# Four weight units of each later expert pair loaded as transfers of 112, 8 and 8 partitions instead of one of 128

## The chip, the cores and the metric

The kernel runs on one core of one Trainium2 chip. The metric is the device time of one execution in microseconds (us), lower being better. The kernel before has a median of 1338.05 us over three runs (1337.34 to 1338.09).

## What is computed

Two layers on a sequence of 256 tokens with 1024 features, all in float32. The first layer is a gated linear recurrence followed by a dense SwiGLU of inner width 3584. The second is a forgetting attention followed by a mixture of eight SwiGLU experts, of which each token uses two. The change touches only that last part:

```python
def moe_swiglu(h, router, w_gate, w_up, w_down):
    logits = (t @ router).astype(jnp.float32)
    top_v, top_i = lax.top_k(logits, TOP_K)             # TOP_K = 2 of N_EXPERTS = 8
    w = jax.nn.softmax(top_v, axis=-1)
    combine = jnp.sum(jax.nn.one_hot(top_i, N_EXPERTS) * w[..., None], axis=1)
    for e in range(N_EXPERTS):
        out = out + combine[:, e:e + 1] * swiglu(t, w_gate[e], w_up[e], w_down[e])
```

Each expert has a gate and an up matrix of 1024 x 3584 and a down matrix of 3584 x 1024, 14 MiB each, so the eight experts are 336 MiB of weights, each read once.

## The kernel before

The front of the kernel (the recurrence, the dense part and the attention) streams its weights in 1 MiB units through six places called `raw` and takes up to about 500 us. The experts come after it. Their tokens are gathered by routing into groups of 32 slots: a "large" expert of a pair has three groups, a "small" one two. Experts are worked in pairs, four pairs for this input: an opening pair, a second one, one in a loop and a last one, each described by an object `Group`.

An expert's weights are read in units of 128 rows by 3584 floats (14,336 bytes in each of 128 partitions, 1.75 MiB). There are eight units for the gate matrix ("G"), eight for up ("U") and eight for down ("D"; `PARTS` is 8). Within the list of a pair (`UNITS`, 48 entries, built by `pair_units`) the kinds alternate, with the down units of the pair's small expert postponed into the next pair. After the last pair a list of eight down units remains (`LAST_UNITS`).

The units go through a ring of eight places (`RING`, `PERMANENT`; three more are used in the opening). The order is strict. SyncE runs `pair_loads`: for each unit it waits until TensorE has finished with the place (`used` against `group.free(i)`), then `load` issues one DMA of the whole unit. That DMA adds 16 to the semaphore `arrived` of its place when it has landed. SyncE does nothing else in this part until the output. TensorE takes the units in the same order: `summed` for a gate or up unit, `lowered` for a down unit. Each starts with a wait on `arrived` of its place against `group.landed(i)`, then issues the unit's matmuls and adds one to `used` at the end of the last one. For each group of slots a gate or up unit is multiplied in four strips of 512 + 384 columns; a down unit is multiplied in pieces of 256 columns. ScalarE and VectorE apply the activation and the routing weights between the stages. The program is written out by hand in this order; no planner places anything.

The wait that the transfer ends, in `summed` and `lowered` alike (lines 1251 and 1267), and the issue itself (line 420):

```python
pe.wait_ge(arrived[group.slot(i)], group.landed(i))
...
sp.dma_start(dst, src).then_inc(arrived[group.slot(i)], 16)
```

Of the kernel before, what the change touches and what calls it, by code (L numbers as in the profile page):

```python
# [22 lines left out]
P = 128  # L23
# [68 lines left out]
def at(count, per, i):  # L92

    return count if i is None else i * per + count
# [7 lines left out]
def pair_units(opening):  # L102

    def sums(kind, job):
        return [(kind, job, n) for n in range(KT)]
    early, late = (range(EARLY), range(EARLY, PARTS))
    return (sums("G", LARGE) + ([] if opening else downs(EARLIER, early)) + sums("U", LARGE)
            + ([] if opening else downs(EARLIER, late)) + sums("G", SMALL) + downs(LARGE, early)
            + sums("U", SMALL) + downs(LARGE, range(EARLY, PARTS)))


OPENING_UNITS, UNITS = pair_units(True), pair_units(False)
LAST_UNITS = downs(EARLIER, range(PARTS))
PAIR_UNITS = len(UNITS)
assert PAIR_UNITS % RING == 0 and len(OPENED) == RING + 3


class Group:


# [20 lines left out]
    def slot(self, i):  # L141
        n = self.later(i)
        return OPENED[n] if n < 0 else PERMANENT[n % RING]

    def landed(self, i):
        n = self.later(i)
        return 16 if n < 0 else at(16 * (n // RING + 2), 16 * PAIR_UNITS // RING, self.i)
# [21 lines left out]
def hybrid_trunk(nc, x, norm_mix, norm_ffn, lru_w_in, lru_conv_w, lru_conv_b, lru_w_a, lru_b_a, lru_w_x, lru_b_x,  # L169
                 lru_log_lambda, lru_w_out, fox_w_in, fox_b_f, fox_q_gain, fox_k_gain, fox_w_out, ffn_w_gate,  # L170
                 ffn_w_up, ffn_w_down, moe_router, moe_w_gate, moe_w_up, moe_w_down, out):
    with ExitStack() as ctx:
        def sem(name):
            return ctx.enter_context(nc.semaphore(name))
# [124 lines left out]
        def strip(c):  # L299
            return slice(c * SLOTS, (c + 1) * SLOTS)  # L300
# [47 lines left out]
            sem(s) for s in ("m_act", "m_aT", "m_acc", "m_S", "m_Sw", "m_col", "m_tab", "m_fin"))  # L348
        arrived = [sem(f"arrived{i}") for i in range(len(OPENED))]
        out_done, sumsq_v, par_in2, ff_T = sem("out_done"), sem("sumsq_v"), sem("par_in2"), sem("ff_T")  # L350
        h_f_done, xn_act = sem("h_f_done"), sem("xn_act")


# [42 lines left out]
        @block.sync  # L396
        def _(sp):
            for t in range(TT):
                sp.dma_start(X[:, t], x[0, t * P:(t + 1) * P, :]).then_inc(x_in, 16)
            for load in par_loads[4:]:  # L400
                sp.dma_start(*load).then_inc(par_in2, 16)
            for n, (w, rows, col) in enumerate(front_units()):
                if n == RR:
                    sp.wait_ge(used, 1)
                elif n > RR:
                    sp.wait_ge(lo_done, max(m for m in range(n) if DENSE[m] == DENSE[n]))
                sp.dma_start(raw[:, DENSE[n]].rearrange("p (k n) -> p k n", k=UK), unit_of(w, rows, col)
                             ).then_inc(landed[DENSE[n]], 16)
                if n == 4:
                    sp.dma_start(wax[:, 0], lru_w_a[0].rearrange("h i j -> i h j")).then_inc(wax_in, 16)  # L410
                    sp.dma_start(wax[:, 1], lru_w_x[0].rearrange("h i j -> i h j")).then_inc(wax_in, 16)

            def load(group, i, expert):
                kind, job, n = group.table[i]
                dst = places[group.slot(i)]
                if kind == "D":
                    src = expert_w[2][expert].rearrange("o (p r) n -> p (o r n)", r=ROWS)[:, n * PLACE:(n + 1) * PLACE]
                else:
                    src = expert_w["GU".index(kind)][expert, n * P:(n + 1) * P, :].rearrange("o p n -> p (o n)")
                sp.dma_start(dst, src).then_inc(arrived[group.slot(i)], 16)  # L420

            def pair_loads(group):
                experts = {LARGE: slice(FIRST, FIRST + 1)} if group is OPENING else {}
                for i, (kind, job, n) in enumerate(group.table):
                    if group is OPENING and i < len(OPENED):
                        continue
                    if job not in experts:
                        if group is OPENING:
                            sp.wait_ge(listed, 1)
                        col = group.col(-1) + 1 if job == EARLIER else group.col() + job  # L430
                        experts[job] = bass.ds(sp.value_load(ids[0:1, bass.ds(col, 1)], min_val=0, max_val=E - 1), 1)
                    sp.wait_ge(used, group.free(i))
                    load(group, i, experts[job])

            def dense_done(*places):
                for place in places:
                    n = last_dense(place)
                    if place < RR:
                        sp.wait_ge(lo_done, n)
                    else:  # L440
                        sp.wait_ge(used, n + 1)

            def open_unit(i):
                load(OPENING, i, slice(FIRST, FIRST + 1))

            dense_done(2, 3, 4, 5)
            open_unit(0)
            open_unit(1)
            sp.wait_ge(scored, 8)
            open_unit(2)  # L450
            dense_done(0, 1, 2)
            open_unit(3)
            sp.wait_ge(o_T, 4)
            open_unit(4)
            dense_done(11, 12)
            open_unit(5)
            dense_done(6, 7)
            open_unit(6)
            dense_done(7, 8, 9)
            open_unit(7)  # L460
            dense_done(9, 10, 11)
            open_unit(8)
            sp.wait_ge(routed, 1)
            open_unit(9)
            sp.wait_ge(hn_hi_done, 2)
            sp.wait_ge(hn_lo_done, 2)
            open_unit(10)
            pair_loads(OPENING)
            pair_loads(SECOND)
            sp.wait_ge(counted, 1)  # L470
            loops = sp.value_load(nblk_i[0:1, 0:1], min_val=LOOPS, max_val=LOOPS_MAX)
            with sp.Fori(0, loops) as n:
                pair_loads(Group(n, 2))
            pair_loads(Group(loops, 2))
            pair_loads(Group(loops, 3, LAST_UNITS))
            for n in range(4):
                j, t = n // 2, n % 2
                sp.wait_ge(m_fin, n + 1)
                sp.dma_start(out[0, t * P:(t + 1) * P, j * CW:(j + 1) * CW], X[:, t, j * CW:(j + 1) * CW]
                             ).then_inc(out_done, 16)  # L480
            sp.wait_ge(out_done, 64)
# [348 lines left out]
        def _(pe):  # L830
# [416 lines left out]
            def summed(group, kind, job, n):  # L1247

                i = group.place[kind, job, n]
                w = places[group.slot(i)]  # L1250
                pe.wait_ge(arrived[group.slot(i)], group.landed(i))
                for a in range(GROUPS[job]):
                    if n == 0:
                        acc_free(group, kind, job, a)
                    x = xg[:, n, FIRST_SLOT[job] + a * SLOTS:FIRST_SLOT[job] + (a + 1) * SLOTS]
                    for b, first, width in PIECES:
                        for c in range(STRIPS):
                            ins = mm(ps[strip(c), 2 * a + b, 0:width], x, w[:, c * STRIP + first:c * STRIP + first + width],  # L1258
                                     start=n == 0, stop=n == KT - 1, skip_group_check=True)
                    if n == KT - 1 and a < GROUPS[job] - 1:  # L1260
                        ins.then_inc(m_part, 1)
                ins.then_inc(used, 1)

            def lowered(group, job, n):

                i, small = group.place["D", job, n], min(job, SMALL)
                pe.wait_ge(arrived[group.slot(i)], group.landed(i))
                at_place = n * PLACE
                for r in range(at_place // D, (at_place + PLACE) // D):
                    for a in range(GROUPS[small]):  # L1270
                        for c in range(STRIPS):
                            at_row = r * D + c * QUARTER
                            held_in = i if at_row >= at_place else i - 1
                            first = at_row - at_place + (i - held_in) * PLACE
                            ins = mm(ps[strip(c), 6 + a // 2, quarter(a % 2)], aTs[small][:, r, held(a)],  # L1275
                                     places[group.slot(held_in)][:, first:first + QUARTER],
                                     start=r == 0 and a % 2 == 0, stop=r == ROWS - 1, skip_group_check=True)
                    if r * D < at_place:
                        ins.then_inc(used, 1)
                if (at_place + PLACE) % D == 0:  # L1280
                    ins.then_inc(used, 1)
# [684 lines left out]
```

## Time and profile before

| | before |
|---|---|
| median of three runs | 1338.05 us |
| profiled execution, device time | 1338.2 us |
| its span, first to last instruction | 1336.4 us |
| granted TensorE clock, mean | 0.998 |
| PE busy | 1271.3 us (95%) |
| LDWEIGHTS busy | 766.0 us (57%) |
| DVE, ACT, POOL busy | 363.3, 284.5, 30.9 us |
| DMA | 435.53 MB, mean 326 GB/s |
| HBM read, written | 432.69 MB, 1.05 MB |
| chain that ended last | PE 73%, DMA 23%, ACT 2%, DVE 1% |

The device time holds the span and about 2 us around it. Busy shares are of the span. The rates of the DMA row are those of all 16 DMA engines together; "share of 16 engines" is the time that packets took, over 16 times the stretch, and it can come out slightly over 100% as packets overlap at their ends.

### The profile page before, as it was taken

The numbers are of one execution on the slowest core, as the hardware profiler recorded it, in microseconds if no ns is written. First come the engines' busy times: TensorE is split into PE (matmuls) and PEld (weight loads), VectorE is DVE, ScalarE is ACT, GpSimd is POOL, SyncE is SP. The second block draws the span as 40 slices with busy tenths as digits, with TensorE's granted clock in tenths as the row PEclk, the third lists the DMA queues.
The fourth block names the chain that finished last, engine by engine and source line by source line (L and its number), as shares of the span: only waits on it lengthen the run. The fifth ranks groups of instructions, "written<-read, shape, count | busy, mean of one in ns | idle before, by whom it ended". The sixth has DMA issues, their size and how long they took to land.

```text
span 1336.4 us, 27795 instructions
## 1 busy us (share of the span) xinstructions
PE 1271.3 (95%) x12897; PEld 766.0 (57%) x12897; DVE 363.3 (27%) x470; ACT 284.5 (21%) x357; POOL 30.9 (2%) x34
## 2 busy tenths in 40 slices
PE   7999999999999999999999999899998799989897
PEld 7978888888888884335534434344344254344344
DVE  6976444445654363020100200100110100020010
ACT  5855444443545530000000000000000000000000
POOL 2000000000230000000000000000000000000000
PEclk9999999999999999999999999999999999999999
DMA  9556555554441298899999999999999999999994
GB/s 338 171 167 227 185 184 184 188 188 157 157 127 64 87 424 339 319 401 425 426 425 425 425 425 425 427 424 426 426 424 426 426 425 426 425 425 425 425 425 198
DMA packets 70323, 435.53 MB, mean 326 GB/s; under 512 B 4656, under 2 KB 6816, under 8 KB 45632
## 3 DMA queue, kind: packets, MB, share of 16 engines
q1 hardware_dynamic: 69744, 433.10, 81.0%
q8 instruction: 101, 1.65, 0.5%
q0 software_dynamic: 368, 0.63, 0.2%
q14 instruction: 14, 0.11, 0.0%
q10 hardware_dynamic: 96, 0.03, 0.0%
HBM read 432.69 MB, written 1.05 MB: 325 GB/s over the span
## 4 chain that ended last, share of the span: by engine, by line
PE 73%; DMA 23%; ACT 2%; DVE 1%; issue 1%; SPq 0%; POOL 0%; DVEq 0%; ACTq 0%
PE ps L1258 25%; DMA ring<-in_moe_w_down_dram 16%; PE ps L1275 13%; PE ps L839 9%; PE ps L841 9%; PE ps L840 9%; DMA ring<-in_moe_w_gate_dram 6%; PE ps L1229 1%; PE ps L1069 1%; PE ps L1096 1%; PE ps L855 1%; PE ps L881 1%; PE ps L871 1%; PE ps L868 1%; PE ps L870 1%
## 5 line engine op out<-in xcount | busy, mean ns | idle before, releaser
L1258 PE MATMUL ps<-ring,xg 128*32 128x512 f32 (+1 forms) x4384 | 423.1, 540 | 26.6 <-DMA ring<-in_moe_w_up_dram 16.1
L1258 PEld LDWEIGHTS ps<-ring,xg 128*32 128x32 f32 x4384 | 140.1, 110 | 299.6 <-issue 251.3
L1423 DVE TENSOR_TENSOR wlo<-raw,whi 128x2048 fp32r<-128x2048 f32 x73 | 166.5, 2287 | 74.2 <-PE ps L841 72.2
L541 ACT ACTIVATE whi<-raw 128x2048 fp32r<-128x2048 f32 x73 | 139.3, 1916 | 85.3 <-PE ps L841 83.8
L839 PE MATMUL ps<-whi,hT_hi 128*128 128x512 f32 x384 | 153.4, 399 | 2.4 <-DVE wlo L1423 1.4
L841 PE MATMUL ps<-whi,hT_lo 128*128 128x512 f32 x384 | 149.9, 390 | 0.0
L840 PE MATMUL ps<-wlo,hT_hi 128*128 128x512 f32 x384 | 149.7, 390 | 0.0
L1275 PE MATMUL ps<-ring,aTL 128*32 128x256 f32 x2352 | 133.9, 380 | 7.3 <-DMA ring<-in_moe_w_down_dram 7.1
L1903 DVE TENSOR_TENSOR gtL<-gtL,ps 128x896 f32<-128x896 f32 x12 | 13.1, 1089 | 368.3 <-PE ps L1258 368.3
L1275 PEld LDWEIGHTS ps<-ring,aTL 128*32 128x32 f32 x2352 | 77.6, 110 | 59.8 <-DMA ring<-in_moe_w_down_dram 7.8
L1275 PE MATMUL ps<-ring,aTS 128*32 128x256 f32 x1568 | 90.2, 380 | 10.7 <-DMA ring<-in_moe_w_down_dram 9.7
L839 PEld LDWEIGHTS ps<-whi,hT_hi 128*128 128x128 f32 x384 | 72.2, 188 | 18.3 <-issue 3.1
L841 PEld LDWEIGHTS ps<-whi,hT_lo 128*128 128x128 f32 x384 | 72.1, 188 | 15.3
L840 PEld LDWEIGHTS ps<-wlo,hT_hi 128*128 128x128 f32 x384 | 72.3, 188 | 13.7
L1275 PEld LDWEIGHTS ps<-ring,aTS 128*32 128x32 f32 x1568 | 51.9, 110 | 46.9 <-DMA ring<-in_moe_w_down_dram 14.1
L1258 PE MATMUL ps<-ring_last,xg 128*32 128x512 f32 (+1 forms) x592 | 58.5, 540 | 3.2 <-DMA ring_last<-in_moe_w_up_dram 3.2
L1903 DVE TENSOR_TENSOR gtS<-gtS,ps 128x896 f32<-128x896 f32 x8 | 8.7, 1087 | 176.3 <-PE ps L1258 176.3
L795 ACT ACTIVATE yS<-ps 128x512 f32<-128x512 f32 x4 | 2.4, 597 | 217.1 <-PE ps L1275 217.1
L839 PE MATMUL ps<-whi,fT_hi 128*128 128x512 f32 x112 | 44.9, 401 | 0.0
L840 PE MATMUL ps<-wlo,fT_hi 128*128 128x512 f32 x112 | 44.3, 395 | 0.0
L841 PE MATMUL ps<-whi,fT_lo 128*128 128x512 f32 x112 | 44.3, 395 | 0.0
L1258 PEld LDWEIGHTS ps<-ring_last,xg 128*32 128x32 f32 x592 | 18.8, 110 | 40.2 <-issue 34.9
(292 smaller groups left out, 1016.9 us busy)
## 6 DMA issues: line engine op xcount, KB each, us to landing
ring<-in_moe_w_down_dram SPq DMA_DIRECT2D x56, 1792.0 KB, 29.1
ring<-in_moe_w_gate_dram SPq DMA_DIRECT2D x55, 1792.0 KB, 27.5
ring<-in_moe_w_up_dram SPq DMA_DIRECT2D x55, 1792.0 KB, 24.8
raw<-in_fox_w_in_dram SPq DMA_DIRECT2D x16, 1024.0 KB, 5.4
raw<-in_ffn_w_gate_dram SPq DMA_DIRECT2D x14, 1024.0 KB, 5.1
raw<-in_ffn_w_up_dram SPq DMA_DIRECT2D x14, 1024.0 KB, 5.1
raw<-in_ffn_w_down_dram SPq DMA_DIRECT2D x14, 1024.0 KB, 5.1
ring_last<-in_moe_w_up_dram SPq DMA_DIRECT2D x8, 1792.0 KB, 27.3
```

The costliest lines, as they stand in the source:

```text
L541: nc.scalar.activation(whi[:, m % HR], raw[:, DENSE[m]], ACT.Copy).then_inc(hi_done, 1)
L839: mm(dst(t), hi, whi[:, m % HR, k * CW:(k + 1) * CW], start=first and k == 0, stop=False)
L840: mm(dst(t), hi, wlo[:, m % LR, k * CW:(k + 1) * CW], start=False, stop=False)
L841: ins = mm(dst(t), lo, whi[:, m % HR, k * CW:(k + 1) * CW], start=False, stop=last and k == UK - 1)
L855: ins = mm(dst, raw[:, 0, k * CW + c * P:k * CW + (c + 1) * P], h_f[:, k], start=k == 0 and c % 2 == 0, stop=False, skip_group_check=True)
L868: mm(dst, wh, hT_hi[:, kk], start=half == 0 and k == 0 and c % 2 == 0, stop=False, skip_group_check=True)
L870: mm(dst, wh, hT_lo[:, kk], start=False, stop=False, skip_group_check=True)
L871: ins = mm(dst, wl, hT_hi[:, kk], start=False, stop=half == 1 and k == UK - 1, skip_group_check=True)
L1258: ins = mm(ps[strip(c), 2 * a + b, 0:width], x, w[:, c * STRIP + first:c * STRIP + first + width], start=n == 0, stop=n == KT - 1, skip_gr ...
L1275: ins = mm(ps[strip(c), 6 + a // 2, quarter(a % 2)], aTs[small][:, r, held(a)], places[group.slot(held_in)][:, first:first + QUARTER], sta ...
L1423: nc.vector.tensor_tensor(wlo[:, m % LR], raw[:, DENSE[m]], whi[:, m % HR].bitcast(F32), ALU.subtract).then_inc(lo_done, 1)
L1903: nc.vector.tensor_tensor(gts[job][:, a], gts[job][:, a], of_group(a), ALU.mult).then_inc(m_act, 1)
```

## The change

Within the lists of the second, the looped and the last pair, the units at places 0, 12, 24 and 36 are loaded by three DMAs. The first carries partitions 0 to 111 and adds to `arrived` as before. The other two carry partitions 112 to 119 and 120 to 127 and add 16 each to one new semaphore, `rest_in`. TensorE waits for both semaphores before such a unit. All other units, those of the opening pair and the eight after the last pair are loaded as before. The bytes and their places in memory are the same.

```diff
+UNEVEN = range(0, PAIR_UNITS, 12)
+TOP, STEP = 112, 8
...
+    def uneven(self, i):
+        return self.table is UNITS and i in UNEVEN
+
+    def rest(self, i):
+
+        per = 16 * (P - TOP) // STEP
+        return at(per * (len(UNEVEN) * (self.ahead - 1) + UNEVEN.index(i) + 1), per * len(UNEVEN), self.i)
...
+        rest_in = sem("rest_in")
...
-                sp.dma_start(dst, src).then_inc(arrived[group.slot(i)], 16)
+                if not group.uneven(i):
+                    sp.dma_start(dst, src).then_inc(arrived[group.slot(i)], 16)
+                    return
+                sp.dma_start(dst[0:TOP], src[0:TOP]).then_inc(arrived[group.slot(i)], 16)
+                for p in range(TOP, P, STEP):
+                    sp.dma_start(dst[p:p + STEP], src[p:p + STEP]).then_inc(rest_in, 16)
...
                 pe.wait_ge(arrived[group.slot(i)], group.landed(i))
+                if group.uneven(i):
+                    pe.wait_ge(rest_in, group.rest(i))
```

The last two lines stand in `summed` and in `lowered`.

## Rows read from the trace of the kernel before

**Rows 1.** the page's 40 slices of 33.4 us; digits are tenths busy

```profile
PE   7999999999999999999999999899998799989897
...
PEclk9999999999999999999999999999999999999999
DMA  9556555554441298899999999999999999999994
GB/s 338 171 167 227 185 184 184 188 188 157 157 127 64 87 424 339 319 401 425 426 425 425 425 425 425 427 424 426 426 424 426 426 425 426 425 425 425 425 425 198
```

**Rows 2.** the page's DMA queues: packets, MB, share of 16 engines' time

```profile
q1 hardware_dynamic: 69744, 433.10, 81.0%
q8 instruction: 101, 1.65, 0.5%
```

**Rows 3.** transfers, 600 to 1300 us: packets by size, then the queues

```profile
DMA packets 23343, 297.66 MB, mean 425 GB/s; under 512 B 2588, under 2 KB 2588, under 8 KB 2588
...
q1 hardware_dynamic: 23269, 296.49, 100.1%
q8 instruction: 69, 1.13, 0.7%
```

**Rows 4.** TensorE's waits, 600 to 1300 us: total us, times, longest us

```profile
PE ps L1258 <- DMA ring<-in_moe_w_up_dram: 16.1, 14, 1.4
PE ps L1275 <- DMA ring<-in_moe_w_down_dram: 12.5, 14, 1.5
PE ps L1258 <- DMA ring<-in_moe_w_gate_dram: 10.5, 12, 1.4
PE ps L1258 <- DMA ring_last<-in_moe_w_up_dram: 3.2, 3, 1.1
```

**Rows 5.** chain of waits, 500 to 1336 us: start us, us, what

```profile
777.96 30.98 DMA ring<-in_moe_w_down_dram
...
987.14 32.24 DMA ring<-in_moe_w_down_dram
...
1197.50 31.06 DMA ring<-in_moe_w_down_dram
```

**Rows 6.** end of the chain, 1170 to 1336 us, same columns

```profile
1296.10 29.33 DMA ring<-in_moe_w_down_dram
...
1325.47 3.71 PE ps L1275 x64
...
1333.22 0.66 DVE X L1937 x2
```

**Rows 7.** stretches of 2 us at the end; last columns DMA share, GB/s

```profile
1306.00:1308.00 2.00, 2.00 (x40) 1.19 (x40) 0.00 (x0) 0.00 (x0) 0.00 (x0) 1.00 1.01 430
1308.00:1310.00 2.00, 2.00 (x45) 1.18 (x37) 0.00 (x0) 0.00 (x0) 0.00 (x0) 1.00 0.67 287
1310.00:1312.00 2.00, 2.00 (x44) 1.23 (x40) 0.00 (x0) 0.00 (x0) 0.00 (x0) 1.00 0.54 223
...
1320.00:1322.00 2.00, 1.38 (x29) 0.60 (x24) 0.00 (x0) 0.00 (x0) 0.00 (x0) 1.00 0.54 216
1322.00:1324.00 2.00, 1.85 (x36) 0.85 (x28) 0.00 (x0) 0.00 (x0) 0.00 (x0) 1.00 0.27 115
1324.00:1326.00 2.00, 0.53 (x12) 0.35 (x16) 0.00 (x0) 0.00 (x0) 0.00 (x0) 1.00 0.03 14
```

**Rows 8.** the tile ring: one issue's ns min/median/max, and us to landing

```profile
L420 SPq DMA_DIRECT2D ring<-in_moe_w_down_dram x56: 328/333/339, 583.8 to 1296.1; - x56
...
DMA to landing us min/median/max: 7.1/27.9/32.5
```

**Rows 9.** SyncE's waits, 600 to 1300 us: total us, times, longest us

```profile
SPq L420 <- PE ps L1258: 387.0, 107, 7.2
SPq L420 <- PE ps L1275: 222.2, 56, 8.1
```

**Rows 10.** a transfer of 8 partitions at the start, in the whole span's issues

```profile
par_rows<-in_lru_conv_b_dram ACTq DMA_DIRECT2D x1, 4.0 KB
```

More of the change, by code:

```diff
@@ L1267, in lowered @@
                 pe.wait_ge(arrived[group.slot(i)], group.landed(i))
+                if group.uneven(i):
+                    pe.wait_ge(rest_in, group.rest(i))
                 at_place = n * PLACE
```

## The prediction

> **What bounds the kernel now.** I read the page's slices first. From slice 18 on (about 600 us) the DMA row is 9 in every slice and the rate stands at 424 to 427 GB/s up to the last slice, while PE swings between 8 and 9 [rows 1]. The clock row is 9 throughout, so the clock plays no part. The queues come second: one queue (q1, the SyncE issues) carries 433.10 MB of the whole span's traffic, and beside it stands a small instruction queue, q8, with 101 packets and 1.65 MB [rows 2]. In 600 to 1300 us, q1 fills 100.1% of the time of the 16 DMA engines [rows 3]. Nothing is left there to be better overlapped: more bytes per us can't be had on average.
>
> TensorE is close behind. In the same 700 us it waits for weight landings only 16.1 + 12.5 + 10.5 + 3.2 = 42.3 us, in 43 short waits of at most 1.5 us [rows 4], so each pair of experts ends with the weight stream and TensorE has about 12 us to spare in each. The chain of waits then goes in a loop: TensorE frees a place, SyncE issues, and the transfer lands 31 to 32 us later; at 128 rows over 16 engines (4.34 us, worked out below) that is seven units deep in the queue. The same point of the pair recurs in it at 777.96, 987.14 and 1197.50 us, every 209.2 and 210.4 us [rows 5]. The last of it is a transfer of the down weights that lands at 1325.43 us, and TensorE starts at once (1325.47); behind it comes a fixed tail of 1336.4 - 1325.4 = 11.0 us [rows 6].
>
> The row that matters for this change comes last. If all 16 engines were in step, the DMA share would fall from 1 to 0 within a few us at the end of the stream. It does not: it is 1.01 in 1306 to 1308, falls to 0.67 and then stands at 0.54 to 0.49 down to 1322, with 0.27 and 0.03 after that [rows 7]. So half of the engines, eight, run out of work at about 1309.5, and the other eight go on until 1322 to 1325. The gap is about 1322 - 1309.5 = 12.5 us. Yet every transfer gives each engine the same bytes: 128 rows, one packet each (23343 - 2588 packets for 297.66 MB, 14.34 KB each, is a weight row of 3584 floats) [rows 3]. The likely load on only eight of them is the instruction queue: 69 packets in 700 us at 0.7% of 16 engines' time [rows 3], 78 us in all, or 1.14 us each. On eight engines that is 9.8 us each in 700 us, which is about the gap that has built up. It is a reading, since no row says on which engine a packet ran. A unit is usable only when its slowest engine has landed, so the kernel pays the slow eight's time.
>
> **The change part by part.** The price of one row on one engine: 16 x 700 x 1.001 us over 296.49 MB / 14336 B = 20,682 rows is 0.542 us [rows 3], so a unit takes 8 x 0.542 = 4.34 us.
>
> *Rows moved between engines.* A 128-row transfer gives each engine 8 rows. 112 rows over 16 engines give 7. A transfer of 8 rows can occupy at most eight engines, with one row each. If the two short ones both take the same eight (call them the short-transfer eight), those carry 9 rows of such a unit and the others 7. Places 0, 12, 24 and 36 of the 48 units of a pair are cut so, in the three pairs after the opening one: 12 units. So the one eight gains 12 x 0.542 = 6.5 us of work and the other loses 6.5 us.
> By a rule of the Trainium skill (DMA: Bandwidth & Descriptors, "Why a DMA increments its semaphore by 16 and not by 1") a transfer runs on the largest number of engines up to 16 that divides its outermost dimension, and takes the lowest-numbered ones, which would be 16 for 112 rows and the same first eight for both short transfers. No run here shows it yet.
> If the eight that lose rows are the slow eight, their end goes from 1325.4 to 1318.9, and the others' from 1309.5 to 1312.5 (with a spread of 3 us like that of the slow eight) up to 1316 to 1319. The two meet, and the last landing comes earlier by half the gap, 12.5 / 2 = 6.2 us: 1319.2. If they are the fast eight, the end goes 6.5 us later. For what comes in between I take -6.2 and keep both signs.
>
> *Does the gain reach the end?* TensorE has 42.3 us of waits to give in 600 to 1300 [rows 4], seven times the gain, and the last wait before the tail is one for a landing [rows 6]. All the time from the first cut unit to the last lies in the full stretch [rows 1]. The gain grows by about 2.1 us per pair, so every landing wait shrinks evenly. What is late next is the other eight: their lead is used up almost exactly, and one more cut unit would bring nothing.
>
> *Two more issues per cut unit.* An issue on SyncE takes 0.333 us [rows 8]: 24 more are 8.0 us, beside 387.0 + 222.2 us in which SyncE waits for TensorE in the 700 us [rows 9]. The short transfers are issued 0.33 and 0.67 us after the long one, and the median transfer lands 27.9 us after its issue [rows 8], behind six others, so the queue hides it. Cost 0; with the cover gone it would be 12 x 0.67 = 8.0 us.
>
> *More semaphore packets and one more wait.* Each transfer ends in a small packet on each of its engines (2588 under 512 B in 700 us [rows 3], 16 per 128-row unit). A cut unit adds 16 on the short-transfer eight. The 0.542 us per row above already holds one such packet for eight rows, so were all of the difference between a row's share and its bytes theirs, it would stay far under a row: 24 of them on each engine of that eight cost between 0 and, at an eighth of a row (0.07 us), 1.6 us. I take 0, since they fall on engines with a lead. The added TensorE wait is satisfied with or before the unit's own landing, as the short rows are queued right behind the long part; 12 waits of 0.04 us, the chain's usual "issue" step, would be 0.5 us, and less than nothing can't come of it. I take 0.
>
> *The row's own price.* All rows above come from transfers of 128 partitions, where 16 engines reach all of them at full rate. The only few-partition transfers of the trace are the parameter loads at the start, 4 KB for 8 partitions, with no landing time of its own [rows 10]. So the cost of an 8-row transfer of 112 KB is bounded from below by 0.542 us (each row on its own engine at full rate) and from above by eight rows one after the other, 4.3 us. The long part is bounded by 7 x 0.542 = 3.8 us and by twice that, should pairs of engines meet on the same partitions. I take the lower ends, being the only durations that the trace has, and keep the upper for a rival.
>
> **Sum.** Against the profiled execution (1338.2 us, span 1336.4): -6.2 + 0 + 0 + 0, so 1332.0, and against the median of 1338.05, 1331.9 us.
>
> **The rivals.**
> (A) Short transfers share their way into memory; slower. Eight rows that go to neighbouring partitions may have to take turns, four engines at a time. Then each of the two short transfers holds its eight engines 4 x 0.542 = 2.2 us in place of 0.54, 3.25 us more per cut unit, 39 us over 12. The point from which it decides: the short-transfer eight have about 6.2 us each to give, 0.5 us per cut unit; one row time more per unit and the gain is gone. In full it gives -6.2 + 39 = +33, 1371 us; with engines that are out of step by 1 to 3 us (the last landings spread over 1322 to 1325 [rows 7]) about half, +13, 1351 us. If the long part meets conflicts too, up to 45 us more. For it: nothing in the rows excludes it. Against it: in the full stretch the rate doesn't dip though engines drift apart by up to 12 us [rows 1, 7], but there each engine has rows of its own, so that says little.
> A page of the Trainium skill speaks for it (SBUF — State Buffer, "Door 1: The DMA port swizzle"): partitions are reached through 16 ports in groups of four, and a transfer gets no more rate than its ports, about 27 GB/s each, so that 8 neighbouring partitions have two ports. Its figure would make a short transfer 8 x 14336 B / 54 GB/s = 2.1 us by estimate.
> (B) The wrong eight; slower. If the instruction packets ride on the short-transfer eight, the slow end grows by 12 x 0.542: 1344.6 us. The rows can't tell; the size of the shift, which is just half the gap, suits the right side but proves nothing.
> (C) No difference. The short transfers are spread over all engines, or half of (A) eats the gain: 1337 to 1339. For it: the trace shows no transfer that leaves engines out.
>
> **How the numbers follow.** The forecast, right eight and full-rate rows: 0.46, at 1331.9, itself between 1330 and 1335. (A) 0.30, most of it at 1342 to 1370. (B) 0.11. (C) 0.13. About 0.2% (2.7 us) is what a measurement can tell here, so faster than 1335.4 is 0.47, slower than 1340.7 0.40, between 0.13. The range of 1330 to 1362 holds the forecast, (C), (B) and the milder two thirds of (A).
>
> **What would show it.** After the change: in the end stretches the DMA share stays near 1 until about 1316 and then falls to 0 within 3 us, with no plateau at 0.5; the last landing is near 1319; the pair period is near 207 to 208 us; TensorE's waits shrink by about 6 us. A plateau of some 25 us would be (B). Under (A) q1's rate in 600 to 1300 falls below 420 GB/s while its share stays at 100%, and waits appear at the cut units, of 2 us and more. I am wrong if the time is above 1335.4.

## The result and the profile after

The changed kernel took 1490.97 us (median of four runs, 1484.72 to 1501.9) against 1337.69 us (1336.94 to 1338.09) for the kernel before on the same chip: ratio 1.1155, with an interval of 1.1087 to 1.1224. It is 153 us slower, or 12.8 us for each of the twelve cut units. The profiled execution took 1493.51 us, its span 1491.8 us.

The page after, in the parts that answer to [rows 1, 2]:

```profile
PE 1316.5 (88%) x12897; PEld 777.9 (52%) x12897; DVE 362.7 (24%) x470; ACT 284.7 (19%) x357; POOL 30.9 (2%) x34
...
PEclk9999999999999999999898999989899899989999
DMA  9465565644316989999999999999999999999992
GB/s 341 143 201 194 184 198 183 196 147 153 100 53 277 403 309 363 425 347 425 331 380 356 310 410 285 388 313 331 370 300 384 277 374 289 348 340 338 373 418 119
...
q1 hardware_dynamic: 69936, 433.10, 82.4%
q8 instruction: 101, 1.65, 0.5%
...
PE 53%; DMA 42%; DVE 2%; ACT 2%; issue 1%; SPq 0%; POOL 0%; DVEq 0%; ACTq 0%
```

Bytes and instruction fetches are as before. The DMA row is still 9 everywhere, yet the rate, a flat 425 GB/s before, falls to between 277 and 388 in most slices. DMA's part of the chain has gone from 23% to 42%. The queues in 600 to 1450 us, against [rows 3]:

```profile
DMA packets 23662, 299.25 MB, mean 352 GB/s; under 512 B 2796, under 2 KB 2796, under 8 KB 2796
...
q1 hardware_dynamic: 23588, 298.09, 100.0%
q8 instruction: 68, 1.11, 0.6%
```

Busy for 100.0% of the time at 352 GB/s instead of 425: engines never lack work, their packets take longer. That is worth 850 x (1 - 352/425) = 146 us of the 155 by which the profiled execution is longer (1493.5 against 1338.2 us). TensorE's waits in 600 to 1490 us, which answer to [rows 4] (L1278 is the old L1258, L1297 the old L1275):

```profile
PE ps L1297 <- DMA ring<-in_moe_w_down_dram: 70.2, 32, 6.3
PE ps L1278 <- DMA ring<-in_moe_w_up_dram: 36.2, 18, 5.6
PE ps L1278 <- DMA ring<-in_moe_w_gate_dram: 26.6, 10, 5.9
```

Single waits are up to 6.3 us long, against 1.5 us before. Short stretches of the changed kernel show where the rate is lost (columns as in [rows 7]; the last three are granted clock, DMA share and GB/s). The first cut unit is issued at 640.21 us, the second at 694.80, the fifth at 882.53, the ninth at 1153.19, the twelfth at 1354.36:

```profile
640.00:656.00 16.00, 16.00 (x204) 7.85 (x200) 5.77 (x4) 0.70 (x1) 0.00 (x0) 1.00 1.01 425
...
660.00:664.00 4.00, 4.00 (x56) 3.01 (x52) 0.00 (x0) 0.70 (x1) 0.00 (x0) 1.00 0.93 201
664.00:668.00 4.00, 4.00 (x80) 2.37 (x76) 0.00 (x0) 0.00 (x0) 0.00 (x0) 1.00 1.02 204
...
656.00:672.00 16.00, 15.65 (x268) 9.71 (x259) 0.00 (x0) 1.00 (x2) 0.00 (x0) 1.00 1.01 243
672.00:712.00 40.00, 40.00 (x460) 17.98 (x464) 0.00 (x0) 3.27 (x4) 0.00 (x0) 1.00 1.00 424
712.00:732.00 20.00, 10.94 (x156) 5.48 (x148) 0.00 (x0) 0.00 (x0) 0.00 (x0) 0.83 1.01 253
...
896.00:928.00 32.00, 24.86 (x368) 15.16 (x368) 3.96 (x3) 2.22 (x3) 0.00 (x0) 0.95 1.00 261
...
1156.00:1200.00 44.00, 34.36 (x444) 17.60 (x436) 5.64 (x4) 1.58 (x3) 0.00 (x0) 0.88 1.01 278
...
1360.00:1376.00 16.00, 7.05 (x68) 2.11 (x64) 0.00 (x0) 1.83 (x2) 0.00 (x0) 0.89 1.00 236
1376.00:1384.00 8.00, 7.59 (x144) 4.69 (x139) 0.00 (x0) 0.00 (x0) 0.00 (x0) 1.00 1.00 389
1384.00:1396.00 12.00, 11.05 (x224) 6.72 (x212) 0.00 (x0) 0.60 (x1) 0.00 (x0) 1.00 1.01 287
```

Every cut unit leaves a dip. The first two begin 16 and some 20 us after the issue, when the unit's turn in the queue comes; the twelfth begins only some 6 us after it and ends some 42 us after it. So by then some engines reach a unit soon after its issue, and others much later. At the floor of a dip the rate is some 200 GB/s, half of 425, with all 16 engines busy. After the first dip it is back at 424. The rate missing in a dip gives its cost: the first, 16 x (425 - 243)/425 = 6.9 us; the second, 20 x (425 - 253)/425 = 8.1; the fifth (896 to 928), 32 x (425 - 261)/425 = 12.3; the ninth (1156 to 1200), 44 x (425 - 278)/425 = 15.2; the twelfth, 7.1 + 0.7 + 3.9 = 11.7 from the last three rows. So later cuts cost about twice the first, and the twelfth dip has two humps, which begin 24 us apart.

The end, against [rows 6, 7]:

```profile
1454.00:1456.00 2.00, 1.56 (x31) 0.70 (x24) 0.00 (x0) 0.00 (x0) 0.00 (x0) 1.00 1.00 423
1458.00:1460.00 2.00, 2.00 (x40) 1.45 (x36) 0.00 (x0) 0.00 (x0) 0.00 (x0) 1.00 0.47 195
1462.00:1464.00 2.00, 2.00 (x44) 1.23 (x40) 0.00 (x0) 0.00 (x0) 0.00 (x0) 1.00 0.21 87
1470.00:1472.00 2.00, 0.74 (x16) 0.17 (x8) 0.00 (x0) 0.00 (x0) 0.00 (x0) 1.00 0.18 79
1478.00:1480.00 2.00, 1.29 (x24) 0.52 (x16) 0.00 (x0) 0.00 (x0) 0.00 (x0) 1.00 0.07 29
```

```profile
1451.11 29.60 DMA ring<-in_moe_w_down_dram
...
1480.75 3.70 PE ps L1297 x64
...
1488.49 0.66 DVE X L1959 x2
```

Most engines now run dry near 1458, but three of 16 (0.18 to 0.21) go on to the last landing at 1480.71: the gap is some 23 us, against 16 before (1309.5 to 1325.4). These 7 us and the 146 of the lower rate make 153 of the 155. The tail behind the last landing is the old 11 us.

### The profile page after: what moved, and what is told of

Read it like the earlier page. It is cut to its first block, busy times and chain, and to the rows that moved or that the text cites. A ratio compares the mean times of both kernels' runs of the same rounds, so it can differ in the third digit from the quotient of the medians.

```text
span 1491.8 us, 27864 instructions
## 1 busy us (share of the span) xinstructions
PE 1316.5 (88%) x12897; PEld 777.9 (52%) x12897; DVE 362.7 (24%) x470; ACT 284.7 (19%) x357; POOL 30.9 (2%) x34
## 4 chain that ended last, share of the span: by engine, by line
PE 53%; DMA 42%; DVE 2%; ACT 2%; issue 1%; SPq 0%; POOL 0%; DVEq 0%; ACTq 0%
PE ps L1278 20%; DMA ring<-in_moe_w_up_dram 17%; DMA ring<-in_moe_w_gate_dram 16%; DMA ring<-in_moe_w_down_dram 9%; PE ps L857 8%; PE ps L859 8%; PE ps L858 8%; PE ps L1297 3%; PE ps L1087 1%; DVE wlo L1445 1%; PE ps L1114 1%; PE ps L899 0%; PE ps L1210 0%; PE ps L1318 0%; PE ps L976 0%
## 5 line engine op out<-in xcount | busy, mean ns | idle before, releaser
L1278 PE MATMUL ps<-ring,xg 128*32 128x512 f32 (+1 forms) x4384 | 444.9, 563 | 74.7 <-DMA ring<-in_moe_w_up_dram 36.2
L1278 PEld LDWEIGHTS ps<-ring,xg 128*32 128x32 f32 x4384 | 147.4, 114 | 363.4 <-issue 305.2
L1297 PE MATMUL ps<-ring,aTL 128*32 128x256 f32 x2352 | 139.5, 391 | 21.6 <-DMA ring<-in_moe_w_down_dram 21.5
L1297 PE MATMUL ps<-ring,aTS 128*32 128x256 f32 x1568 | 103.0, 414 | 36.2 <-DMA ring<-in_moe_w_down_dram 35.2
L1297 PEld LDWEIGHTS ps<-ring,aTL 128*32 128x32 f32 x2352 | 79.2, 113 | 78.5 <-DMA ring<-in_moe_w_down_dram 17.5
L1297 PEld LDWEIGHTS ps<-ring,aTS 128*32 128x32 f32 x1568 | 54.9, 119 | 82.0 <-DMA ring<-in_moe_w_down_dram 39.5
L1278 PE MATMUL ps<-ring_last,xg 128*32 128x512 f32 (+1 forms) x592 | 58.5, 540 | 4.0 <-DMA ring_last<-in_moe_w_up_dram 4.0
L818 ACT ACTIVATE ST<-ps 128x768 f32<-128x768 f32 (+1 forms) x8 | 5.6, 704 | 185.6 <-PE ps L1338 185.6
## 6 DMA issues: line engine op xcount, KB each, us to landing
ring<-in_moe_w_gate_dram SPq DMA_DIRECT2D x49, 1792.0 KB, 33.4
```

Of the source, the lines that this page charges most:

```text
L818: nc.scalar.activation(ST[:, first:first + n].rearrange("p a t -> p (a t)"), flat(4, n * T), ACT.Copy).then_inc(m_ST, 1)
```

## The experiments

Each edit is against the changed kernel. Runs whose names begin with e are the kernel with another form of loading; m1 and m2 are programs that only load. The kernel before had medians of 1337.19, 1338.16 and 1337.75 us beside the three sets of runs, in which the experiments stand as e1 to e4; e5 to e7 and m1; e8, e10, e11 and m2.

**Two short transfers as one, and equal halves.**

```diff
-TOP, STEP = 112, 8
+TOP, STEP = 112, 16      # e1
+TOP, STEP = 64, 64       # e2
```

> The 12 cut units are loaded as 112 + 16 partitions, with no transfer of 8. If the long part is what costs (seven rows per engine no longer lie where eight did, so that engines meet on the same partitions' way into memory), most of the 153 us stays: 1430 to 1490 us, with dips of the DMA rate to 200-300 GB/s at every cut unit. If the two short transfers on eight engines cost (my rival A in its first form, 39 us), the dips go and the time is 1338 to 1350 us, since 112 + 16 gives every engine 8 rows again.

> The 12 cut units are loaded as two transfers of 64 partitions. Every engine still gets 8 rows and there is one more issue per unit. If what counts is only rows per engine and the number of transfers, nothing changes: 1336 to 1341 us. If engines share ways into memory, and 64 neighbouring partitions reach only half of the ways, each half runs at half rate: at least 4.3 us more per cut unit, 12 x 4.3 = 52 us, and more when the engines are out of step: 1390 to 1450 us.

e1 took 1473.06 us, +136; e2 took 1493.94 us, +157, above the 1450 that I gave as its upper end. Each is one run, but the differences are far above what a run varies. With one short transfer less, nearly all of the loss remains; with no short transfer at all, and eight rows on each engine, it is all there. So the eight-row transfers are not the main cost, nor is the uneven number of rows.

**The long part alone.** The two short transfers and their wait are taken out; 16 rows of each of the 12 units are not loaded.

> The change without the two short transfers: at the 12 places only partitions 0 to 111 are loaded, 16 rows of each are left out. It moves 12 x 0.54 = 6.5 us less per engine. If the long part alone makes the cost: 1450 to 1475 us, near the 1473 of 112 + 16 less a few us. If the short transfers hold up the rest by their 2.1 us rows (as they do alone): 1400 us or less.

1450.58 us, one run: +113 though 12 units are an eighth smaller, which is worth 12 x 0.542 = 6.5 us. The long part by itself makes about three quarters of the loss.

**Two transfers, cut in other directions.** e5 cuts by columns (all 128 partitions in each half), e8 takes every second partition (64 in each, as e2 has).

```diff
# e5
+sp.dma_start(dst[:, 0:WHOLE], src[:, 0:WHOLE]).then_inc(arrived[group.slot(i)], 16)
+sp.dma_start(dst[:, WHOLE:], src[:, WHOLE:]).then_inc(rest_in, 16)
# e8
+sp.dma_start(dst[0:P:2], src[0:P:2]).then_inc(arrived[group.slot(i)], 16)
+sp.dma_start(dst[1:P:2], src[1:P:2]).then_inc(rest_in, 16)
```

> At the 12 places the unit comes in two transfers of all 128 partitions and half of the columns each: as many transfers, issues and bytes per transfer as 64 + 64 partitions, and rows half as long. If cutting a unit in two costs by itself (issue, semaphore packets, shorter packets), a good part of the 157 us of 64 + 64 shows here. If only the partitions of a transfer count: 1337 to 1340 us, below 2 us more.

> At the 12 places the unit comes in two transfers of 64 partitions, the even ones and the odd ones, in place of 0-63 and 64-127 (1493.9 us). If a shape that runs at full rate alone (64 partitions two apart took 31.3 us for 14) costs nothing here either: 1337 to 1341 us. If each engine must write where it does in whole units, or it meets the others once they are out of step: 1345 to 1400 us.

e5: 1338.53 us, ratio 1.0003 (0.9993 to 1.0013). e8: 1338.09 us, ratio 1.0003 (0.9993 to 1.0013). The same 16 us, in which the first cut unit passes, in e2 and then in e8:

```profile
656.00:672.00 16.00, 14.80 (x252) 9.15 (x240) 0.00 (x0) 1.51 (x2) 0.00 (x0) 1.00 0.99 231
```

```profile
656.00:672.00 16.00, 16.00 (x272) 10.06 (x268) 0.00 (x0) 1.02 (x2) 0.00 (x0) 1.00 1.00 421
```

231 against 421 GB/s, with two transfers of 64 rows, one more issue and one more wait in both. Cutting in two costs nothing; which partitions stand together in a transfer decides. Each transfer reads from HBM the rows of the partitions that it writes, here and in all runs, so no run tells the writing side from the reading side. Against the reading side speaks only that whole down units, whose pieces lie 114,688 bytes apart in memory, stream at the same 425 GB/s as gate and up units, whose pieces lie side by side [rows 1].

**The shapes by themselves.** m1 only loads: thirteen phases of 14 units (the last of 7), each drained before the next, with nothing else on the chip's queues.

> Only loads, no computing: the program runs thirteen phases of loads of the expert weights (rows of 14,336 bytes) one after the other and copies x to the output; everything else is left out. Each phase issues 14 transfers of one shape to 14 places and waits for all. By rows per engine alone (0.542 us a row): 128 partitions 61 us, 112 53 us, 0-63 30 us, 0-95 46 us, 8 neighbours 7.6 us (112-119), 8 partitions four apart 7.6 us (0-28 and 64-92), 4 neighbours 7.6 us, 4 partitions four apart 7.6 us, 64 partitions two apart 30 us, 8 partitions sixteen apart 7.6 us; then seven cut units of 112 + 8 + 8, 30 to 34 us. If four neighbouring partitions (and those 32 further) share one way into memory at one engine's rate: 128 still 61 us and the partitions four apart still 7.6 us, but 0-63 61 us, 8 neighbours 30 us, 4 neighbours 30 us, 8 sixteen apart 15 us, and 112 between 61 and 107 us.

Its steady stretches (columns: POOL busy, clock, DMA share, GB/s), in order: partitions 0 to 127; 0 to 111; 0 to 63; 0 to 95; 112 to 119; then 0 to 28 by fours; 0 to 3; 0 to 126 by twos; seven cut units of 112 + 8 + 8.

```profile
10.00:60.00 50.00, 0.00 (x0) 1.00 1.01 429
75.00:145.00 70.00, 0.00 (x0) 1.00 1.01 275
160.00:210.00 50.00, 0.00 (x0) 1.00 1.01 208
225.00:290.00 65.00, 0.00 (x0) 1.00 1.01 248
300.00:325.00 25.00, 0.00 (x0) 1.00 0.47 50
328.00:338.00 10.00, 0.00 (x0) 1.00 0.41 138
...
355.00:380.00 25.00, 0.00 (x0) 1.00 0.24 25
...
462.00:490.00 28.00, 0.00 (x0) 1.00 0.95 405
...
510.00:572.00 62.00, 0.00 (x0) 1.00 0.90 200
```

With a share of 1.01, all 16 engines busy, 112 partitions get 275 GB/s, 96 get 248, the lower 64 get 208, and 64 taken by twos 405. Eight neighbours keep half of the engines busy (0.47) for 50 GB/s; eight partitions four apart, at much the same share, get 138, and there SyncE, with 0.7 us per issue, may set the pace. Four neighbours get 25 GB/s, so two groups of four get 50. Per unit, the 112 rows take 1.606 MB / 275 = 5.8 us, against 7 x 0.542 = 3.8. An eight-row transfer takes 0.115 MB / 50 = 2.3 us, against 0.542. A whole cut unit takes 1.835 MB / 200 = 9.2 us, against 4.3: +4.9. Alone, then, the two short transfers lose more (3.5 us) than the long one (2.0).

A page of the Trainium skill (SBUF — State Buffer, "Door 1: The DMA port swizzle") has partitions in groups of four on 16 ports of some 27 GB/s, with partitions 32 apart on the same port, so that 0 to 63 reach half of the ports and get at most about 218 GB/s. The 208, 50 and 25 GB/s above agree with it.

**Fewer cuts.** e7 cuts only the unit at place 0 of the three pairs (`UNEVEN = range(0, 12, 12)`).

> The change with only place 0 of each later pair cut (3 units instead of 12). If each cut unit costs the same, 153 / 4 = 38 us more: about 1376 us. If a cut costs more the further the engines have drifted apart, and the cuts themselves drive them apart, less than a quarter: 1350 to 1368 us.

1369.79 us, one run: +31.6, or 10.5 us per cut. Its three dips:

```profile
656.00:672.00 16.00, 15.04 (x256) 9.36 (x251) 0.00 (x0) 1.51 (x2) 0.00 (x0) 1.00 1.00 226
868.00:892.00 24.00, 18.45 (x293) 11.68 (x291) 0.00 (x0) 2.22 (x3) 0.00 (x0) 1.00 1.00 239
1084.00:1116.00 32.00, 24.61 (x368) 14.75 (x368) 4.11 (x3) 2.22 (x3) 0.00 (x0) 0.95 1.01 242
```

The rate missing is worth 7.5, 10.5 and 13.8 us, and their sum of 31.8 is the whole loss. The same three units cost 6.9, 12.3 and 15.2 us in the changed kernel, where three more cuts lie between each and the next. So a cut costs more the later it comes, and most of that growth is there without the cuts between. The kernel before has half of its engines 16 us ahead at the end; a lead that builds up through the stream would explain the growth, but only its end is seen.

**Engines out of step.** m2 only loads: phases of six whole units, X and five whole ones, with X whole, 112 + 8 + 8, 112 + 16, or by twos; each once in step and once after 16 rows that only eight of the engines carry.

> Only loads again; everything else is left out. Eight phases: 6 whole units, one unit loaded in some form, 5 whole units; the form is whole, 112 + 8 + 8, 112 + 16, or two transfers of every second partition; each once with all engines in step, and once after 16 rows that only eight engines carry (partitions four apart, 8.6 us), so that those start late. From the shapes alone: whole 12 x 4.4 = 53 us, 112 + 8 + 8 4.7 us more, 112 + 16 about 3.8 us more, every second partition 0 to 0.2 us more; started late, each 8.6 us longer. If a cut costs the same whatever the engines' lags, the started-late phases exceed the whole one (61.6 us) by the same 4.7, 3.8 and 0.2 us. If engines out of step meet on each other's partitions for as long as the lag lasts, they exceed it by more: 8 us and above for 112 + 8 + 8, and some us even for every second partition.

The first phase is issued from 0.73 us on. SyncE's first issues of the second to the fifth:

```profile
55.23 15.19 SPq L193 DMA_DIRECT2D place<-in_moe_w_gate_dram  x22
```

```profile
122.56 14.92 SPq L193 DMA_DIRECT2D place<-in_moe_w_gate_dram  x14
```

```profile
182.83 15.36 SPq L193 DMA_DIRECT2D place<-in_moe_w_gate_dram  x23
```

```profile
257.69 16.25 SPq L193 DMA_DIRECT2D place<-in_moe_w_gate_dram  x13
```

In step, the whole unit's phase lasts 54.5 us and the cut one's 182.83 - 122.56 = 60.3, +5.8. Out of step they last 67.3 and 74.9, +7.5. The same differences for 112 + 16 are +5.1 and +7.2, and by twos +0.1 and -1.4. The lead was to be 16 x 0.542 = 8.7 us. But SyncE issued the 16 short transfers 0.7 us apart, slower than a row's 0.542, so the eight engines nearly kept up: the held-back whole phase is 12.8 us longer than the other, and not 8.7. A lead of 8.7 us would show at its end as a plateau of 0.5 (columns as for m1):

```profile
119.00:120.00 1.00, 0.00 (x0) 1.00 0.61 258
120.00:121.00 1.00, 0.00 (x0) 1.00 0.14 57
121.00:122.00 1.00, 0.00 (x0) 1.00 0.10 43
```

So a lead of at most some 2 us was made. Even so a cut out of step costs some 2 us more, and one that lines up costs nothing more. The direction is the one that the kernel shows; a lead of 12 us and more was never given to a stream without TensorE.

**Which eight are late.** e3 replaces place 36 of three pairs by eight transfers of eight rows, four apart, within partitions 0 to 63; e10 by eight of six rows. The rest of those three units is left out.

```diff
+for n, b in enumerate((0, 1, 2, 3, 32, 33, 34, 35)):
+    rows = slice(b, b + 29, 4)        # e3;  b + 21 in e10
+    sp.dma_start(dst[rows], src[rows]).then_inc(rest_in if n else arrived[group.slot(i)], 16)
```

> Which eight engines lag? In one unit of each of the three later pairs (place 36) partitions 64 to 127 are not loaded at all, and partitions 0 to 63 come in eight transfers of 8 partitions, four apart (0, 4, ... 28 and so on). The short-transfer eight then carry 8 rows as before, the others none: 3 x 8 x 0.542 = 13 us less for those. If those others are the lagging eight (as my forecast had it), the end comes up to the lead of 12.5 us earlier: 1325 to 1328 us. If the short-transfer eight lag, nothing is won: 1337 to 1340 us. If 8-row transfers are slow even with partitions four apart, it is above 1345 us.

> As the run with the upper half left out (1336.2 us), but with transfers of 6 partitions four apart, 8 of them, so that only six engines carry 8 rows of the unit at place 36 and the other ten none (80 of its 128 rows are not loaded). In that earlier run the last two of 16 engines lagged as before, so two of the lagging engines must be among the short-transfer eight. If they are its last two, all lagging engines are relieved now by 3 x 8 rows = 13 us: 1325 to 1329 us. If they are among its first six, 1336 to 1338 us again.

e3: 1336.18 us, ratio 0.9991 (0.9981 to 1.0). e10: 1335.29 us, ratio 0.9981 (0.9972 to 0.9991). The end of e3, then of e10:

```profile
1308.00:1310.00 2.00, 2.00 (x44) 1.20 (x40) 0.00 (x0) 0.00 (x0) 0.00 (x0) 1.00 0.62 259
1310.00:1312.00 2.00, 2.00 (x44) 1.07 (x37) 0.00 (x0) 0.00 (x0) 0.00 (x0) 1.00 0.24 100
...
1320.00:1322.00 2.00, 2.00 (x44) 1.07 (x36) 0.00 (x0) 0.00 (x0) 0.00 (x0) 1.00 0.12 50
```

```profile
1310.00:1312.00 2.00, 2.00 (x41) 1.20 (x41) 0.00 (x0) 0.00 (x0) 0.00 (x0) 1.00 0.12 50
...
1320.00:1322.00 2.00, 1.37 (x28) 0.54 (x19) 0.00 (x0) 0.00 (x0) 0.00 (x0) 1.00 0.07 29
```

Half the load of three units, 24 rows or 13 us, is taken from the eight engines that these rows don't use (fourteen eight-row transfers in a row held a share of 0.47 in m1, so they keep to the same eight). Had all eight late engines been among them, the plateau of 0.54 in [rows 7] would be gone. It falls to 0.12, two of 16. So six of the late engines were relieved, and two carry the eight-row transfers. With six rows per transfer, a share of 0.07 is left at 1320, one of 16. If transfers of six rows run on six of the same eight engines, which no row shows, one late engine is among those six and the other is one of the remaining two. Little was won in time (1.0 and 2.5 us), since a unit is usable only when its last engine has landed.

**A balanced cut.** e4 loads columns 0 to 1791 of place 36 in one transfer, and the rest in 16 transfers of eight partitions four apart; e6 uses eight neighbours instead.

```diff
+sp.dma_start(dst[:, 0:WHOLE], src[:, 0:WHOLE]).then_inc(arrived[group.slot(i)], 16)
+for b in [h + b for h in (0, 32, 64, 96) for b in range(4)]:     # e6: for b in range(0, P, 8)
+    rows = slice(b, b + 29, 4)                                    # e6: slice(b, b + 8, 1)
+    sp.dma_start(dst[rows, WHOLE:], src[rows, WHOLE:]).then_inc(rest_in, 16)
```

> The same balance as my forecast wanted, without a transfer of 112: at place 36 of the three later pairs, columns 0 to 1791 of the unit come in one transfer of 128 partitions, and the other half of the columns in 16 transfers of 8 partitions, four apart. The short-transfer eight carry 12 rows' worth, the others 4; over three units 12 rows = 6.5 us are moved. If an engine's rows are its only cost, -6 us: 1331 to 1333 us. If each way into memory is already full with the rows of the engine that owns it, what the short-transfer eight write for the others slows those by as much as it relieves them: no gain, 1338 to 1350 us. 56 and more transfers of slow issue would show as idle DMA engines, not expected.

> As the run with the columns apart (1356 us), but each of the 16 short transfers takes 8 neighbouring partitions instead of 8 that lie four apart. Same bytes, same engines by number, same issues. By the engines alone: 1356 us again. If neighbours share a way into memory, each short transfer takes 4 rows' time instead of one, half a row each: 16 x 3 x 0.27 = 13 us more on eight engines per cut unit, 39 us over three: 1380 to 1400 us.

e4: 1356.29 us, ratio 1.0146 (1.0129 to 1.0163), so 6 us per such unit and above both of the ranges expected. e6: 1361.25 us in one run, 5 us more, between its two. In e4 the engines are never idle (share 1.01 from 600 to 1300 us) but get 418 and then 416 GB/s, which is worth 14 of the 19 us. My reading is that the short-transfer eight then write also to partitions that the other eight serve; it isn't separated from the rows of half the length. e6 costs far less than full turn-taking would; SyncE's 16 issues may set the pace there, which wasn't separated either.

## Why the prediction was wrong

The forecast was 1331.9 us, in a range of 1330 to 1362; measured was 1491. Rival (A) had the right kind of mechanism, transfers that don't reach their full rate, but laid it on the wrong part, and its price was off too.

- *What bounds the kernel.* Right: the stream of weights sets the time. TensorE's waits for landings went from 42 us (600 to 1300) to 133 us (600 to 1490) in the groups shown, and the end moved by what the stream lost.
- *The row's own price: the failed step.* "I take the lower ends, being the only durations that the trace has." The long part was taken at 7 x 0.542 = 3.8 us; alone it takes 5.8. A short transfer was taken at 0.542 us; alone it takes 2.3. The bounds written beside them, 7.6 and 4.3 us, hold both of these prices. The reason given for the lower ends was no reason: every row of the trace is a 128-partition transfer, so none is near to the new shapes. But the prices alone would have given only 1338 - 6 + 12 x 4.9 = 1391 us, and even both upper bounds, 11.3 us more per cut unit, stay under the 12.8 measured. The sum had no term for the whole units that share the stream with a cut one; that is the other 100 us.
- *Rival (A)* laid the cost on the short transfers (+39), with the long part as an afterthought of "up to 45". In the kernel it is the other way round: e11 has about 113 of the 153 us with the long part alone. And even the two together, 84 us, fall short of 153, since they count only the cut unit's own rows. The fifth dip passes 32 x 261 = 8.4 MB, four and a half units, below the full rate, so whole units next to a cut one are slowed as well: the first dip costs 6.9 us, later ones 8 to 15.
- *"With engines that are out of step ... about half".* Wrong in sign. I thought that a lead keeps rows from meeting. What the runs show is that whole units, halves by columns (e5) and every second partition (e8) cost nothing in a stream whose engines end 16 us apart, and that a contiguous cut costs more out of step: 7.5, 10.5 and 13.8 us in e7 from the early cut to the late one, two humps 24 us apart in the twelfth dip, +2 us in m2. My reading is that in a whole unit each engine has its partitions to itself, that with 112 rows an engine's rows lie in part where another engine writes, and that a lead lengthens the time in which some engine is in such a unit. No row says which engine wrote where, so this stays argued. The end gap has grown from 16 to 23 us, so the cuts add to the lead. Why the cost rises from 7 to 15 us isn't settled in its size: no run set the lead of a late cut by itself.
- *Rows moved between engines.* Wrong too, but small. The gap was taken as 12.5 us; to the last landing it is 16. By e3 two of the late eight are among the engines that carry the short transfers, so at full-rate rows the end would have gone about 6.5 us later, as in (B), and not 6.2 earlier. The forecast would have failed even if every row had come at the full rate. That the instruction queue makes eight engines late was tested by no run.
- *Two more issues, one more wait, more semaphore packets: 0.* Right as far as tested: e5 and e8 have one more issue and wait per cut unit and are level with the kernel before. The first cut unit's long issue takes 0.35 us on SyncE and the two short ones 0.80 us together, about what was assumed.
- *"The clock plays no part."* True of the kernel before; after, it is 0.960 on average. In 720 to 724 us TensorE did nothing, and its clock was then 0.50, the lower of its two levels, in 724 to 728:

```profile
720.00:724.00 4.00, 0.00 (x0) 0.00 (x0) 0.00 (x0) 0.00 (x0) 0.00 (x0) 0.74 0.97 194
724.00:728.00 4.00, 3.71 (x36) 1.78 (x40) 0.00 (x0) 0.00 (x0) 0.00 (x0) 0.50 0.99 204
```

PE's busy time rises from 1271.3 to 1316.5 us. This follows from the waits and isn't their cause: q1 stays at 100.0%, so TensorE did not hold the stream back for long.

The signs named for (A) all came: q1's rate under 420 GB/s at a share of 100%, and waits of 2 us and more behind each cut unit but the first, in whose dip TensorE waited only 0.35 us.

## What to carry to other kernels

When a large transfer is cut in two, the cost is in which partitions (and so which rows) each piece covers, and not in the number of pieces: cut along the columns, or take every second partition, and leave a contiguous run of 112, 96 or 64 partitions alone if the stream is saturated. When a trace holds no transfer of the new shape, its cheapest row is no estimate of it; a load-only kernel with one phase per shape gives the price within one run, and the price in a full stream can be more than twice that, because its neighbours pay too. A DMA share of 100% says that engines are busy, not that they are fast: read GB/s beside it.

## What was not expected of the hardware

- A transfer of 112 partitions runs slower than one of 128, not just in proportion: 275 against 429 GB/s, with all 16 engines busy. 96 get 248 and the lower 64 get 208.
- 64 partitions by twos run at 405 GB/s, nearly twice the rate of 64 neighbours.
- One unit that doesn't line up costs 4.9 us among its like and 5.8 us between whole units, but 7 to 15 us in the kernel, more the later it comes, where engines are up to 23 us out of step at the end.
- The late eight engines of the kernel before are not one half of the 16: by e3 two of them are among the eight that carry eight-row transfers, and six are not. What makes them late is open.
